# A two-model forward pass in one kernel: parts of x read by 256-column matmuls moved 28 bytes

## The reference

```python
gu = hn @ w_ffn_in[l]                                                  # 1024 x 5632
h = h + (jax.nn.silu(gu[..., :FFN_HIDDEN]) * gu[..., FFN_HIDDEN:]) @ w_ffn_out[l]
```

## Time and profile before

| | |
|---|---|
| median of three runs | 1640.84 us (1639.11 to 1642.11) |
| the profiled execution | 1639.45 us |
| its span, first to last instruction | 1637.6 us |
| mean granted TensorE clock | 0.999 |
| read from HBM | 281.00 MB, 172 GB/s over the span |

### The profile page before, as it was taken

The page is one execution under the profiler, slowest core; times in us unless marked ns, Lnnn a source line. Parts: engine busy times, 40 slices in busy tenths (PEclk is TensorE's granted clock), DMA queues, the critical chain, the costliest instruction groups (busy, mean ns, idle before and its releaser), DMA issues.

```text
span 1637.6 us, 27241 instructions
## 1 busy us (share of the span) xinstructions
PE 1619.0 (99%) x11554; PEld 1464.8 (89%) x11554; DVE 1208.4 (74%) x1384; ACT 920.9 (56%) x1229; POOL 183.2 (11%) x127
## 2 busy tenths in 40 slices
PE   8999999999999999999999899999999999999999
PEld 8999989999988888888988698888888898898888
DVE  6888868675588767986576778866887667678864
ACT  7966778445554454444486854444444447864442
POOL 0000000000022101220005002210122000002210
PEclk9999999999999999999999999999999999999999
DMA  7554434544355465545544046545554564245444
GB/s 280 178 188 155 156 129 143 193 162 173 133 206 201 135 201 196 210 174 171 205 171 166 16 166 220 180 156 204 207 196 156 182 224 145 104 172 208 178 159 132
DMA packets 44617, 283.80 MB, mean 173 GB/s; under 512 B 4945, under 2 KB 6609, under 8 KB 17745
## 3 DMA queue, kind: packets, MB, share of 16 engines
q1 hardware_dynamic: 44352, 281.99, 48.8%
q10 hardware_dynamic: 144, 0.08, 0.0%
HBM read 281.00 MB, written 1.05 MB: 172 GB/s over the span
## 4 chain that ended last, share of the span: by engine, by line
PE 91%; ACT 4%; DVE 3%; issue 1%; DMA 0%; ACTq 0%; DVEq 0%
PE bank L529 90%; ACT WH L1232 1%; DVE WL L1820 1%; PE bank L703 1%; ACT SB L1353 0%; DVE STAT L1966 0%; ACT FB L1353 0%; DMA PAR<-in_par 0%; PE bank L1168 0%; ACT XR L1239 0%; DVE FB L2186 0%; DVE FB L2181 0%; ACT TMP L1412 0%; ACT TMP L1312 0%; DVE SB L1961 0%
## 5 line engine op out<-in xcount | busy, mean ns | idle before, releaser
L1820 DVE TENSOR_TENSOR WL<-RAW,WH 128x2048 fp32r<-128x2048 f32 (+2 forms) x280 | 585.1, 2093 | 163.5 <-ACT WH L1232 159.7
L1232 ACT ACTIVATE WH<-RAW 128x2048 fp32r<-128x2048 f32 (+2 forms) x280 | 489.9, 1753 | 308.5 <-PE bank L529 305.4
L529 PE MATMUL bank<-XR,WH 128*128 128x256 f32 (+1 forms) x2608 | 645.6, 326 | 0.5 <-DVE WL L1820 0.5
L529 PE MATMUL bank<-XR,WL 128*128 128x256 f32 x1832 | 514.3, 281 | 0.0
L529 PEld LDWEIGHTS bank<-XR,WH 128*128 128x128 f32 x2608 | 435.1, 188 | 47.8 <-issue 3.7
L529 PEld LDWEIGHTS bank<-XR,WL 128*128 128x128 f32 x1832 | 345.4, 189 | 0.1
L529 PE MATMUL bank<-XF,WH 128*128 128x512 f32 x880 | 305.3, 392 | 0.0
L529 PE MATMUL bank<-XM,WH 128*128 128x512 f32 (+1 forms) x928 | 279.1, 361 | 0.0
L529 PE MATMUL bank<-XF,WL 128*128 128x256 f32 x880 | 246.0, 280 | 0.0
L529 PE MATMUL bank<-XM,WL 128*128 128x256 f32 x800 | 223.7, 280 | 0.0
L529 PEld LDWEIGHTS bank<-XF,WH 128*128 128x128 f32 x880 | 165.2, 188 | 36.5
(11 more groups left out here) (298 smaller groups left out, 1762.7 us busy)
## 6 DMA issues: line engine op xcount, KB each, us to landing
RAW<-in_f1i SPq DMA_DIRECT2D x44, 1024.0 KB, 4.8
RAW<-in_f2i SPq DMA_DIRECT2D x44, 1024.0 KB, 4.8
RAW<-in_w_in SPq DMA_DIRECT2D x35, 1024.0 KB, 4.8
RAW<-in_w_ffn_in SPq DMA_DIRECT2D x22, 1024.0 KB, 4.8
RAW<-in_f1o SPq DMA_DIRECT2D x32, 704.0 KB, 4.2
RAW<-in_f2o SPq DMA_DIRECT2D x32, 704.0 KB, 4.1
RAW<-in_diff_w_in SPq DMA_DIRECT2D x12, 1024.0 KB, 4.9
RAW<-in_w_ffn_out SPq DMA_DIRECT2D x16, 704.0 KB, 4.2
```

What stands on the lines that cost most here:

```text
L529: return e.matmul(o, l, r, start=start, stop=stop)
L1232: e.activation(split_at(u, cols)[0], RAW[:, u % NRAW, 0:cols], ACT.Copy).then_inc(hi_done.tick(u), 1)
L1820: e.tensor_tensor(lo, RAW[:, u % NRAW, 0:cols], hi.bitcast(f32), sub).then_inc(lo_done.tick(u), 1)
```

## The change

The areas XR, XM, XS and XO get 16 more words, and a second view of two parts, 7 words (28 bytes) further on (`parts_of(buf, 7)`): XRT and XMT beside XR and XM; XS and XO have the shifted view alone. All 256-column products read and write the shifted views. The networks keep XR, XM and XF at the old places in their tensors; IN_XR's weights stay in XR, XW and XV stay as they are. FA and FB are shifted by 7 words too, so that the working tiles F(i) lie on the shifted areas, and are 16 words longer. Every tensor behind XR begins 64 bytes further, FB and what shares its memory 128. No instruction, wait or order of a queue is changed.

```diff
--- before.py
+++ after.py
@@ -230,12 +230,16 @@
             SIGNALS.append(s)
             return s
 
+        def parts_of(buf, at):
+            return buf[:, at:at + 2 * 2048].rearrange("p (z c) -> p z c", z=2)
+
         SIGNALS = []
         RAW = sb("RAW", [128, NRAW, 2048])
         WH = sb("WH", [128, NW, 2048], f32r)
         WL = sb("WL", [128, NW, 2048], f32r)
         R0 = sb("R0", [128, 264])
-        XR = sb("XR", [128, 2, 2048], f32r)
+        xr = sb("XR", [128, 2 * 2048 + 16], f32r)
+        XR, XRT = parts_of(xr, 0), parts_of(xr, 7)
         HT = sb("HT", [128, 8, S])
         PAR = sb("PAR", [128, NPAR])
         CON = sb("CON", [128, NCON])
@@ -245,21 +249,23 @@
         TMP = sb("TMP", [128, 3, 512])
         STAT = sb("STAT", [128, 768])
         NA, NB = 4, 5
-        with nc.sbuf_tensor("XM", [128, 2, 2048], f32r) as XM:
+        with nc.sbuf_tensor("XM", [128, 2 * 2048 + 16], f32r) as xm:
+            XM, XMT = parts_of(xm, 0), parts_of(xm, 7)
+        with nc.sbuf_tensor("BELOW_XW", [128, 2 * 2048], f32):
             with nc.sbuf_tensor("XW", [128, 2, 2048], f32r) as XW:
                 pass
-        FA = sb("FA", [128, NA * 2048])
+        FA = sb("FA", [128, NA * 2048 + 16])[:, 7:7 + NA * 2048]
         with nc.sbuf_tensor("XF", [128, 2, FF * 2], f32r) as XF:
             pass
-        with nc.sbuf_tensor("XS", [128, 2, 2048], f32r) as XS:
-            pass
+        with nc.sbuf_tensor("XS", [128, 2 * 2048 + 16], f32r) as xs:
+            XS = parts_of(xs, 7)
         with nc.sbuf_tensor("BEFORE_F7", [128, 2 * 2048], f32):
             with nc.sbuf_tensor("XV", [128, 2048], f32r) as XV:
                 pass
         with nc.sbuf_tensor("BELOW", [128, 3 * 2048], f32):
-            with nc.sbuf_tensor("XO", [128, 2, 2048], f32r) as XO:
-                pass
-        FB = sb("FB", [128, NB * 2048 + 1024 + 2048])
+            with nc.sbuf_tensor("XO", [128, 2 * 2048 + 16], f32r) as xo:
+                XO = parts_of(xo, 7)
+        FB = sb("FB", [128, NB * 2048 + 1024 + 2048 + 16])[:, 7:7 + NB * 2048 + 1024 + 2048]
         EA = FB[:, NB * 2048:NB * 2048 + 3072]
         E0, F0 = EA[:, 0:1024], EA[:, 1024:3072]
         COS, SIN = E0[:, 0:256], E0[:, 256:512]
@@ -416,7 +422,7 @@
         ACC2, SQB = F(1)[:, 0:512], F(1)[:, 512:1024]
         RN = {"mix": R0, "mem": R0, "x": R1, "ffn": R0, "ffn1_0": R1, "mix_0": R0, "ffn2_0": R1, "ffn1_1": R0, "mix_1": R1,
               "ffn2_1": R0}
-        XN = {n: XR for n in RN} | {"x": XS, "ffn2_0": XM, "ffn2_1": XM}
+        XN = {n: XR if n in ("ffn", "ffn1_0", "ffn1_1") else XRT for n in RN} | {"x": XS, "ffn2_0": XM, "ffn2_1": XM}
         GAIN = {"mix": "norm_mix_g", "mem": "norm_mem_g", "x": "norm_x_g", "ffn": "norm_ffn_g"}
         SQX, SQM = F(3), F(9)
         SUM_BEFORE = {"x": "mem", "ffn": "x", "ffn1_0": "ffn", "mix_0": "ffn1_0", "ffn2_0": "mix_0", "ffn1_1": "ffn2_0", "mix_1": "ffn1_1",
@@ -717,7 +723,7 @@
                 empties(key, *events)
 
 
-            xT = two(XR)
+            xT = two(XRT)
 
             def warm():
 
@@ -845,16 +851,16 @@
                 if j < 4:
                     unit_T(("w_br_hgrn", j), two(XS), "ob", 8, (merged, ("b", j)))
                 else:
-                    unit_T(("wkv_x", j - 4), two(XR), "mem", 8, (rscaled, ("kx", j - 4)))
+                    unit_T(("wkv_x", j - 4), two(XRT), "mem", 8, (rscaled, ("kx", j - 4)))
                     if j == 4:
                         norm_sum("mem")
                 moba_steps(36 + j, 1)
             for n in range(4):
                 unit_halves("w_br_attn", n, two(XS), "oa", 4, lambda k: (merged, ("a", k)))
             for k0, k1 in ((0, 6), (6, 7), (7, 8)):
-                out_part("w_out", 0, two(XM), "merged", 8, k0, k1, lambda k: (hrow, ("w_out", k)), "main")
+                out_part("w_out", 0, two(XMT), "merged", 8, k0, k1, lambda k: (hrow, ("w_out", k)), "main")
             for n in range(1, 4):
-                unit_halves("w_out", n, two(XM), "merged", 8, lambda k: (hrow, ("w_out", k)))
+                unit_halves("w_out", n, two(XMT), "merged", 8, lambda k: (hrow, ("w_out", k)))
             qx, kx, vx = tiles(QX, 256), tiles(KX, 256), tiles(VX, D)
 
             def cross_scores(h):
@@ -892,12 +898,12 @@
             for n in range(2, 4):
                 unit_T(("wq_x", n), two(XS), "x", 8, (rscaled, ("qx", n)))
                 cross_scores(n - 2)
-            proj_N("wkv_x", 2, two(XR), "mem", 8, lambda j: (copied, ("vx", 0, j)), lambda n: cross_scores(2 + n))
-            proj_N("wkv_x", 3, two(XR), "mem", 8, lambda j: (copied, ("vx", 1, j)), lambda n: (cross_turn(2 * n), cross_turn(2 * n + 1)))
+            proj_N("wkv_x", 2, two(XRT), "mem", 8, lambda j: (copied, ("vx", 0, j)), lambda n: cross_scores(2 + n))
+            proj_N("wkv_x", 3, two(XRT), "mem", 8, lambda j: (copied, ("vx", 1, j)), lambda n: (cross_turn(2 * n), cross_turn(2 * n + 1)))
             for h in range(4):
                 cross_out(h)
             for n in range(4):
-                unit_halves("wo_x", n, two(XM), "xo", 4, lambda k: (hrow, ("wo_x", k)))
+                unit_halves("wo_x", n, two(XMT), "xo", 4, lambda k: (hrow, ("wo_x", k)))
 
             ffn("ffn", "w_ffn_in", "w_ffn_out")
 
@@ -1558,7 +1564,7 @@
                 for k in (2 * n, 2 * n + 1):
                     q.wait_ge(merged, ("m", k))
                     q.wait_ge(parts, ("oa", 3))
-                    high_part(("merged", k), tiles(GA, 256)[:, k, :], XM, k * 256, 256)
+                    high_part(("merged", k), tiles(GA, 256)[:, k, :], XMT, k * 256, 256)
             out_units("w_out", "x", 1)
             for n in range(4):
                 asked(("wq_x", n))
@@ -1599,7 +1605,7 @@
             asked(("wo_x", 0))
             for h in range(4):
                 q.wait_ge(cross, ("o", h))
-                high_part(("xo", h), in_bank(("xo", h))[:, :], XM, h * 512, 512)
+                high_part(("xo", h), in_bank(("xo", h))[:, :], XMT, h * 512, 512)
             out_units("wo_x", "ffn")
             ffn("ffn", "w_ffn_in", "w_ffn_out", "ffn1_0")
 
@@ -2243,7 +2249,7 @@
                     q.wait_ge(merged, ("a", k))
                     e.tensor_tensor(ga, ga, tiles(MB, 256)[:, k, :], add).then_inc(merged.tick(("m", k)), 1)
                     q.wait_ge(merged, ("m", k))
-                    low_part(("merged", k), ga, XM, k * 256, 256)
+                    low_part(("merged", k), ga, XMT, k * 256, 256)
             asked(("w_br_attn", 3))
             q.wait_ge(small["x"], 0)
             out_units("w_out", "w_out", None, "x", 1)
@@ -2279,7 +2285,7 @@
             asked(("wkv_x", 7))
             asked(("wo_x", 0))
             for h in range(4):
-                low_part(("xo", h), in_bank(("xo", h))[:, :], XM, h * 512, 512)
+                low_part(("xo", h), in_bank(("xo", h))[:, :], XMT, h * 512, 512)
             out_units("wo_x", "wo_x", "w_out", "ffn", 0, True)
             ffn("ffn", "w_ffn_in", "w_ffn_out", "wo_x", "ffn1_0", 1.0)
```

## The result

The changed kernel takes 1646.38 us (median of 6 runs, 1645.63 to 1647.27), the one before 1639.23 (6 runs, 1639.11 to 1642.11): a ratio of 1.0037 [1.0027, 1.0047], which is 6.1 us of 1640. The medians stand 7 us apart, but 33 executions of the kernel before in a later series have a median of 1640.37, and from that it is 6.0. The profiled executions stand 7.8 us apart, 1647.27 against 1639.45. The forecast was 1628 and faster. Lines behind 238 have moved: 529 is 535 now, 1820 is 1826, 1828 is 1834, 1437 is 1443.

A forecast was written before the change was run, and what follows sets the result against it. TensorE's matmul start pace was taken as the bound. Only the shifted 256-column matmuls counted, -12.9 us, all else 0: 1639.45 - 12.9 = 1626.5, plus 1.4 for the median, 1628 us; range 1606 to 1648.

The forecast's parts named there:

- What bounds the kernel: Whole kernel: TensorE busy 1619.0 of 1637.6 us; a projection lasts as long as its matmuls take to be started in turn.
- (e): Next bound if TensorE gets faster: the weights, some 12% away, taking nothing from a 3% gain.
- (c): Networks' matmuls from XR, XF and XM: padding changes nothing, 0 us, ends +-1.6 us.
- (b): Price per shifted 256-column matmul: 3.3 ns cheaper, times 3,900 gives -12.9 us.
- (a): 256-column matmuls outside the networks: 4536, 533 us, 33% of the span; 3,900 taken as setting the end.
- (d): ScalarE, VectorE and GpSimd on areas 28 bytes off: 0 us, covered by TensorE's time; ends 0 and +5 us.
- rival 3: Streamed or stationary x: off-boundary start costs 3.3 ns a matmul, +12.9 us, 1654 us; chance 0.21.
- Rival 2: Shifted matmuls: start inside a line does nothing or costs one more line, +0.6 us, 1641.4 us; chance 0.20.
- only the stationary side pays: Variant of rival 3: only the 864 matmuls with x as stationary operand cost 3.3 ns more, 2.9 us, 1644 us.
- a change in the networks' pair: Sign in the next profile: networks' 512- and 256-column pair leaving 346 ns would prove the reading wrong.

The follow-up runs named there:

- e1: Kernel before plus 64 unused bytes behind XR, nothing shifted; 1651.44 us, ratio 1.0063.
- e6: Changed kernel with a shift of 8 words in place of 7, keeping its 64-byte pads; 1643.65 us, ratio 1.0021 to the kernel before.
- e7: Changed kernel's layout and pads with a shift of 0 words in place of 7; 1644.43 us, ratio 1.0024 to the kernel before.
- e2: Changed kernel with pads of 128 bytes in XR and FA, 28-byte shift kept; 1642.63 us, ratio 1.0011 to the kernel before.
- e5: Changed kernel with a shift of 8 words in place of 7 and 128-byte pads; 1637.96 us, ratio 0.9982 to the kernel before.
- e3: Kernel before, x read 0 to 31 words further on, varying by unit of `w_in` and the networks; one execution, 1649.92 us.
- e9: XR alone read 8 words on, block 0 put 32 bytes nearer than blocks 1 to 7; 1640.17 us, ratio 0.9997 to the kernel before.
- e11: e5 plus short constant matmuls of 8 to 112 columns ahead of units 3 to 16 of the first stretch; one execution, 1638.2 us.
- e8: Changed kernel with an 8-word shift for XR alone, 128-byte pads, other areas not shifted; 1639.14 us, ratio 0.9991 to the kernel before.
- e12: e5 plus only two short constant matmuls, 8 and 16 columns, ahead of units 3 and 4; 1637.60 us, ratio 0.9979 to the kernel before.
- e4: Kernel before, weights read 0 to 31 words further on, varying by unit of `w_in` and the networks; one execution, 1648.56 us.

## Why the prediction was wrong

**What bounds the kernel** was right. TensorE's start-to-start pace sets the projections, padding that touches no other engine moved the end by 10.3 us (e1), and (e), the weights as the next bound, was never reached.

**(c) is the step that failed.** It read that XF "begins 128 and XM 64 bytes further because of the padding, still 32 past a multiple of 64" and took 0 with ends of 1.6 us. The starts had been compared modulo 64, and the runs show that 64 bytes are not nothing: XM at 96 modulo 128 costs 6.6 ns a pair, 4.4 us over 672, in all four kernels that have it there (the changed one, e1, e6 and e7), and XF's 128 bytes cost its pairs nothing (0.05 us from 424 to 824). e1, e2 and e7 show it from three sides: padding alone +10.3 (XM and XF), shift alone +1.8, the change's padding without the shift +4.1. No row could have told 64 from 128, since all areas stood at 32 modulo 128 in the kernel before; but then the support for 0 in (c), XF and XM "at other distances already", did not cover a new start modulo 128 either. An end was at hand: the earlier trace rows has a pair at 352.5 ns, dearer by 6.5, and 6.5 ns x 672 = 4.4 us. That it meets the measured 4.4 is luck, as the next paragraph shows. Why a start at 96 is slow for a pair stays open.

**The two rows that (b) was built on** do not show the price of a start. The prediction took XO on XR's weights and XM on XW's as "just these two cases". But x from XS and XM with the weights in WH ran at 118.7 ns in the same trace, and the same two cases come out otherwise at the same starts: XO on XR's weights in the second mixer, 47 steps in 5.85 - 0.28 us, 118.5 ns for 120, and XM on XW's weights, both at 32 modulo 128, in e2 and e5:

```profile
1445.17 5.85 PE L529 MATMUL bank<-XO,XR 128*128 128x256 f32 x48
...
968.32 5.72 PE L535 MATMUL bank<-XM,XW 128*128 128x512 f32 x32
...
961.85 5.81 PE L535 MATMUL bank<-XM,XW 128*128 128x512 f32 x32
```

The first line is of the kernel before, the second of e2 (347.2 ns a pair), the third of e5 (353.1), as the earlier trace rows. So the 3.3 and 6.5 ns were also one of two paces against the other.

**(b) had the sign wrong and the size too large.** It took -3.3 ns for 3,900 matmuls, -12.9 us. e2, the 28 bytes without the networks' loss, is +1.8 us, 0.5 ns a matmul. The mean steps over whole runs, from the four traces, in ns (steps above 135 left out):

| x | before | after | e2 | e7 |
|---|---|---|---|---|
| streamed from XR | 116.9 | 117.5 | 117.6 | 116.9 |
| stationary, in XR | 118.3 | 119.6 | 119.5 | 118.3 |
| streamed from XS | 118.3 | 117.5 | 118.5 | 117.0 |
| streamed from XM | 118.0 | 118.6 | 117.5 | 118.3 |
| streamed from XO on W | 118.0 | 117.1 | 118.6 | 116.7 |
| streamed from XO on XR's weights | 119.3 | 116.9 | 117.8 | 119.8 |

Only XR keeps its place but for the 28 bytes, and there they cost: 0.6 and 1.3 ns, 2.5 us over 2328 and 864 matmuls. The gain on XS in the changed kernel is not theirs: e7, which has the pads alone, has it too, and e2 has not. "The size of the effect that rows show", 3.3 ns, has its like in the quick pace after a 32-byte step (113.3 in e5, 113.4 in e3, against 116.7), but it was applied to a start that no row had. The argument that "both operands start on 32-byte steps now" and so meet "on their boundaries every time" is not borne out: 7 words gave no quick pace, and where e5 puts both operands on 32-byte steps, a quick pace and a slow one both occur.

**(a)** stands: 33% of the span in these matmuls, and over them the two traces differ by 7.9 - 4.4 - 1.5 = 2 us; the steps in the table times the counts give 1.8.

**(d) and the other engines** were right: 484 and 1910 ns in the groups before and after, and the wait ahead of the first of them 26.9 and 26.8 us.

**The rest**, about 1.5 us in the two profiled executions, is the clock dip at 915 us, 6.8 us at the 1.2 GHz level against 3.4, after TensorE had been idle 2.36 of 3 us (before: 0.83 of 3). The other traces here show one or the other length (3.4 in e5, e9 and e11, 6.8 in e1, e8 and e12). It is not put down to the change, and accounts for most of what lies between the 7.8 us of the two traces and the 6.1 of the ratio.

**The range** reached 1648 and so held the 1646.38, but by luck: its upper end was put together from half of rival 3 and the ends of (c) and (d), 1.6 and 5 us, and none of them is where the 4.4 us arose.

**The rivals.** Rival 3 had the sign, and with "only the stationary side pays", 1644, nearly the time; but its mechanism, 3.3 ns for every x that starts off a boundary, is not what happened: the 28 bytes brought under a third of the loss. Rival 2, drawn from the page "SBUF — State Buffer" of the Trainium skill (Specifications, the line on cachelines of 16 bytes), put the shift at +0.6 us. That rule alone does not carry the runs: 4 and 8 words on are starts on a line as 0 is, and give 118.3 and 113.4 ns against 116.7. By the rule e1, 64 bytes further, would have cost nothing; it cost 10.3 us. In the networks' pairs the place within four words does show, on top of the rest (354 to 360 ns at 1 or 2 words past), but 3 words past, where the 28 bytes put x, was not slow.

The page "TensorE: Matmul & The Clock Gate" of the Trainium skill, Part 2, Step-by-step: what each phase is for, says that the streamed operand and the load of the next weights have separate read ports, so that the load takes no bandwidth from the matmul. e4 is against reading this as independence in time: with x in place in XM, weights 4 words further on made the pair 353.5 ns in all four units tried, against 346.7 at 0. Which read waits for which no trace here shows.

A mark that the prediction set was met: "a change in the networks' pair" would prove the reading wrong, and it did, in the part whose places were thought unchanged.

## What to carry to other kernels

Before anything is padded or shifted, write down where every matmul operand starts modulo 256 bytes, before and after, for the tensors behind the edited one too: here 64 unused bytes in one area cost 10.3 us in areas allocated later. Pad in multiples of 256 bytes, so that an experiment with one operand's place leaves the others where they were: 128 left the networks' pairs alone, but moved 256-column matmuls from XM by 2 ns (e8), while XS in e8 and XM in e9, 256 further, kept their paces. Before a price is read from one row, look for the same kind of row elsewhere in the trace: the 120.0 and 352.5 ns each had a second value at the same starts. And measure a new place in whole runs: 3.3 ns read from a single unit of a scan promised 16 us from 32 bytes, and whole runs gave 2.4.

## What the hardware showed that was not expected

- A stream of float32r matmuls with a weight load each runs at 113.3 to about 122 ns for 256 columns, and a pair of 512 and 256 columns at 346 to 360, depending on where both operands start. For the pair 32 and 160 bytes past a multiple of 256 are alike and 224 is slow; for 256 columns 32 and 160 differ.
- At one and the same set of addresses there are two steady paces that last from unit to unit: 113.3 and 117.8 ns with x 64 bytes past a multiple of 128, 116.7 and 117.8 with XR at 32 in the kernel before, 347.2 and 353.1 for the pairs from XM on XW's weights. The pace changed at a 24-column matmul between two units in e11, at a 16-column one in e12, and in e12 a row 0.12 us longer than its neighbours stands where it went back.
- The worst places of x for the pair are 1 and 2 words past a multiple of 4 words: one word further 359 ns, two words 358.5, against 347 at 0; three words past was not among them (350).
- A start 28 bytes off changed nothing for VectorE (484 ns) or ScalarE (1910 ns).
- The dip of TensorE's clock near 915 us lasts 3.4 or 6.8 us from one execution to another, worth 1.5 us; the traces of e2 and e6 have a second one of 3.4 us, 10 us after the end of the first.
